# The last layer norm's shift row put into the outputs beforehand, and the outputs stored by accumulating transfers

## The reference

```
x = layer_norm(ALPHA * x + gate1 * mix, ln1_g, ln1_b)
ffn = expert_choice_ffn(x * (1 + scale2) + shift2)
y = layer_norm(ALPHA * x + gate2 * ffn, ln2_g, ln2_b)

layer_norm(x, g, b) = (x - mean(x)) * rsqrt(var(x) + 1e-6) * g + b      # mean and var over the 2048 columns
```

## Time and profile before

| | |
|---|---|
| runs of the kernel | 2162.7, 2165.96 and 2167.95 us, median 2165.96 us |
| the profiled execution | 2165.0 us, of which the span from the first to the last instruction is 2163.4 us |
| busy in the span | PE 2042.6 us (94%), DVE 1000.5 us (46%), ACT 202.6 us (9%), POOL 115.4 us (5%) |
| moved by DMA | 649.10 MB, mean 300 GB/s |
| experts (1163 to 2104 us) | DMA engines' busy share 0.99, 421 GB/s |
| from 2137.0 to 2160.2 us | DVE busy 21.81 of 23.20 us, PE 3.46, ACT 3.46, POOL 10.51 |

### The profile page before, as it was taken

How to read it: one execution, slowest core, us unless ns; L and a number is a source line. 1 busy time by engine, 2 the same in 40 slices (tenths; PEclk the granted TensorE clock), 3 DMA queues, 4 the chain that set the end, 5 groups by cost and what they waited for, 6 DMA issues and landing times.

```text
span 2163.4 us, 21990 instructions
## 1 busy us (share of the span) xinstructions
PE 2042.6 (94%) x9427; PEld 1198.9 (55%) x9427; DVE 1000.5 (46%) x1359; ACT 202.6 (9%) x482; POOL 115.4 (5%) x166
## 2 busy tenths in 40 slices
PE   6999999999999999999999999999999999998995
PEld 3455455555799999999784433333333333332221
DVE  3321256638699899898653351121112222222126
ACT  2111310000011111111011200000000000000000
POOL 1010010002010000100100100000000000000001
PEclk8999999999999999999999999999999999999998
DMA  9993027513277666666758799999999999999994
GB/s 342 403 363 117 0 72 263 196 57 107 78 234 241 227 232 230 217 230 229 283 198 348 307 396 433 431 431 431 431 430 431 431 432 430 430 425 436 427 422 178
DMA packets 141851, 649.10 MB, mean 300 GB/s; under 512 B 7314, under 2 KB 83996, under 8 KB 118650
## 3 DMA queue, kind: packets, MB, share of 16 engines
q1 hardware_dynamic: 129698, 586.05, 68.1%
q0 software_dynamic: 11568, 61.57, 8.0%
q10 hardware_dynamic: 488, 0.08, 0.0%
HBM read 641.15 MB, written 6.52 MB: 299 GB/s over the span
## 4 chain that ended last, share of the span: by engine, by line
PE 71%; DMA 19%; DVE 7%; SPq 1%; ACT 1%; issue 1%; DVEq 0%; ACTq 0%
DMA ring<-in_w_up_dram 13%; PE ps L976 12%; PE ps L1310 11%; PE ps L1355 8%; PE ps L1519 8%; PE ps L982 6%; PE ps L1042 4%; DMA ring<-in_w_down_dram 4%; PE ps L1097 3%; PE ps L913 2%; PE ps L785 2%; PE ps L750 1%; PE ps L797 1%; PE ps L1229 1%; DMA ring<-in_w_ada_dram 1%; PE ps L1495 1%
## 5 line engine op out<-in xcount | busy, mean ns | idle before, releaser
L1310 PE MATMUL ps<-ring,arena 128*64 128x512 f32 x2016 | 458.3, 599 | 32.3 <-DMA ring<-in_w_gate_dram 21.7
L1310 PEld LDWEIGHTS ps<-ring,arena 128*64 128x64 f32 x2016 | 140.7, 137 | 337.5 <-issue 273.8
L2564 DVE TENSOR_TENSOR arena<-ps,arena 128x512 f32<-128x512 f32 x180 | 116.0, 686 | 380.2 <-PE ps L1229 380.2
L1355 PE MATMUL ps<-ring,arena 128*64 128x512 f32 x960 | 212.9, 601 | 7.8 <-DMA ring<-in_w_down_dram 6.5
L1901 DVE SCALAR_TENSOR_TENSOR arena<-ring,arena 128x2048 f32<-128x2048 f32 x90 | 211.4, 2349 | 2.1
L976 PE MATMUL ps<-arena,ring 128*128 128x192 f32 x1024 | 174.4, 326 | 0.1
L976 PEld LDWEIGHTS ps<-arena,ring 128*128 128x128 f32 x1024 | 167.6, 190 | 1.5 <-issue 1.2
L1519 PE MATMUL ps<-arena,ring 128*128 128x384 f32 x512 | 165.6, 486 | 0.0
L1355 PEld LDWEIGHTS ps<-ring,arena 128*64 128x64 f32 x960 | 67.9, 138 | 141.1 <-issue 129.1
L1519 PEld LDWEIGHTS ps<-arena,ring 128*128 128x128 f32 x512 | 97.2, 190 | 68.2 <-issue 0.9
L976 PE MATMUL ps<-ring 128*128 128x192 f32 x768 | 132.7, 326 | 0.0
(11 more groups left out here) (381 smaller groups left out, 1831.9 us busy)
## 6 DMA issues: line engine op xcount, KB each, us to landing
ring<-in_w_gate_dram SPq DMA_DIRECT2D x28, 4096.0 KB, 20.4
ring<-in_w_up_dram SPq DMA_DIRECT2D x28, 4096.0 KB, 20.4
ring<-in_w_down_dram SPq DMA_DIRECT2D x28, 4096.0 KB, 20.7
ring<-in_w_in_dram SPq DMA_DIRECT2D x29, 2048.0 KB, 8.7
ring<-in_w_ada_dram POOLq DMA_DIRECT2D x48, 1024.0 KB, 5.2
ring<-in_w_ada_dram SPq DMA_DIRECT2D x32, 1024.0 KB, 17.9
ring<-in_w_out_dram SPq DMA_DIRECT2D x16, 2048.0 KB, 8.9
ring<-in_w_ada_dram SPq DMA_DIRECT2D x8, 2048.0 KB, 13.0
```

The costliest lines, as they stand in the source:

```text
L1310: mm = pe.matmul(ps[j // 4][64 * half:64 * half + m, :], xe_w[g % 2][:, c0:c0 + m], w[:, k4, half * 512:(half + 1) * 512], start=(k == 0), ...
L1355: mm = pe.matmul(ps[3 + u % 2][64 * half:64 * half + 64, :], hidT[:, k % 4, 64 * (k // 4):64 * (k // 4) + 64], w[:, k2, u * 512:(u + 1) * ...
L2564: dve.tensor_tensor(out, ps[SCATTER_BANKS[q % 5]][:, :], out, ALU.add).then_inc(S["cb_used"], 1)
```

## The change

The shift row b no longer goes through an engine at the end. During the gate stage SP writes `ln2_b` into all 384 rows of the two outputs, in three transfers from DRAM to DRAM of 1 MB each, one ahead of each of the loads `ga` 4, 5 and 6. At the end the half tiles, now without b, are stored by transfers that add to what the output holds. They are issued by POOL. DVE does (x - mean) * g for all three tiles, one pass a block, and ACT multiplies each half tile by r (with a bias column of zeros). POOL's four products and sums, DVE's four shifts and the load and the copying of `ln2_b` are gone. ACT takes all three square roots before the first of its six products.

```diff
+                    if kind == "ga" and 4 <= b < 7:
+                        sp.dma_start(out_rows(b - 4), t["ln2_b"][0].partition_broadcast(P)).then_inc(st_ahead, 16)
...
-            for ready, count, tile, half in (("out_mid", 1, 0, 0), ("out_ready", 1, 1, 0), ("out_ready", 2, 1, 1),
-                                             ("out_mid", 2, 0, 1), ("out_ready", 3, 2, 0), ("out_ready", 4, 2, 1)):
-                dst = y_prompt[0] if tile == 0 else y_sample[0, (tile - 1) * P:tile * P, :]
-                cs = slice(half * 1024, (half + 1) * 1024)
-                sp.wait_ge(S[ready], count)
-                sp.dma_start(dst[:, cs], acc[:, tile, cs]).then_inc(st_out, 16)
...
-            pool.dma_start(ln2[0:1, 1, :], row(t["ln2_b"][0], 1)).then_inc(ld_ln2, 16)
-            pool.wait_ge(ld_ln2, 32)
-            for kind in range(2):
-                pool.partition_broadcast(ln2[:, kind, :], ln2[0:1, kind, :]).then_inc(gp, 1)
-            pool.wait_ge(gp, 8)
-            for half in range(2):
-                cs = slice(half * 1024, (half + 1) * 1024)
-                pool.wait_ge(S["scaled_g"], 2 * half + 2)
-                pool.tensor_tensor(acc[:, 0, cs], acc[:, 0, cs], ln2[:, 0, cs], ALU.mult).then_inc(gp, 1)
-                pool.wait_ge(gp, 9 + half)
-                pool.tensor_tensor(acc[:, 0, cs], acc[:, 0, cs], ln2[:, 1, cs], ALU.add).then_inc(S["out_mid"], 1)
+            pool.wait_ge(ld_ln2, 16)
+            pool.partition_broadcast(ln2[:, 0, :], ln2[0:1, 0, :]).then_inc(gp, 1)
+            pool.wait_ge(st_ahead, 112)
+            for tile in range(3):
+                for half in range(2):
+                    cs = slice(half * 1024, (half + 1) * 1024)
+                    pool.wait_ge(S["out_ready"], 2 * tile + half + 1)
+                    pool.dma_start(out_rows(tile)[:, cs], acc[:, tile, cs], accum_op=ALU.add).then_inc(st_out, 16)
...
             for tile in range(3):
                 act.wait_ge(S["var_done"], 4 + tile)
                 act.activation(lnv[:, tile, 2:3], lnv[:, tile, 2:3], ACT.Sqrt).then_inc(S["std_done"], 1)
-                if tile < 2:
-                    act.wait_ge(S["scaled"], 1)
-                    for u in (2 * tile, 2 * tile + 1):
-                        rows = acc[:, 0, u * 512:(u + 1) * 512]
-                        act.activation(rows, ps[LAST_BANKS[0, u]][:, :] if u % 2 else rows, ACT.Identity,
-                                       bias=lnv[:, 0, 4:5], scale=lnv[:, 0, 3:4]).then_inc(S["scaled_g"], 1)
+            for tile in range(3):
+                act.wait_ge(S["scaled"], tile + 1)
+                for half in range(2):
+                    cs = slice(half * 1024, (half + 1) * 1024)
+                    act.wait_ge(S["drained"], 4 * tile + 2 * half + 2)
+                    act.activation(acc[:, tile, cs], acc[:, tile, cs], ACT.Identity,
+                                   bias=iota[:, 0:1], scale=lnv[:, tile, 3:4])\
+                       .then_inc(S["out_ready"], 1)
...
             def last_norms():
                 last_stats(0)
+                dve.wait_ge(gp, 7)
+                last_gain(0, 0)
+                last_gain(0, 1)
                 last_scale(0)
-                link(dve.scalar_tensor_tensor(lnv[:, 0, 4:5], lnv[:, 0, 0:1], -1.0, lnv[:, 0, 3:4], ALU.mult, ALU.mult))
-                dve.sem_inc(S["scaled"], 1)
                 last_stats(1)
-                dve.wait_ge(gp, 8)
-                last_gain(1, 0)
-                last_gain(1, 1)
+                last_gain(0, 2)
+                last_gain(0, 3)
+                last_scale(1)
                 last_stats(2)
-                last_scale(1)
-                last_shift(1, 0)
-                last_gain(1, 2)
-                last_gain(1, 3)
+                for u in range(4):
+                    last_gain(1, u)
                 last_scale(2)
-                last_gain(2, 0)
-                last_shift(1, 1)
-                last_gain(2, 1)
-                last_gain(2, 2)
-                last_shift(2, 0)
-                last_gain(2, 3)
-                last_shift(2, 1)
+                for u in range(4):
+                    last_gain(2, u)
```

More of the change, by code:

```diff
@@ L409, in contexts_of, with out_rows @@
             return ps[CTX_BANKS[k // 4]][:, k % 4 * 64:(k % 4 + 1) * 64].rearrange("p (a b) -> p a b", b=CAP_C)
+        def out_rows(tile):
+            return y_sample[0, (tile - 1) * P:tile * P, :] if tile else y_prompt[0]
         def xe_count(e):
@@ L583, in _ @@
             load_bada(2)
[L585 removed]
+            pool.wait_ge(st_ahead, 64)
             pool.dma_start(ckv[:, 1, :], t["cache_kv_c"][0, 0]).then_inc(ld_att, 16)
@@ L2593, in last_scale @@
                 dve.wait_ge(S["std_done"], 4 + tile)
-                link(dve.reciprocal(lnv[:, tile, 3:4], lnv[:, tile, 2:3]))
+                dve.reciprocal(lnv[:, tile, 3:4], lnv[:, tile, 2:3]).then_inc(S["scaled"], 1)
             def last_gain(tile, u):
@@ L2601, in last_gain @@
                                          ALU.subtract, ALU.mult).then_inc(S["drained"], 1)
-            def last_shift(tile, half):
-                cs = slice(half * 1024, (half + 1) * 1024)
-                dve.wait_ge(S["drained"], 4 * (tile - 1) + 2 * half + 2)
-                dve.scalar_tensor_tensor(acc[:, tile, cs], acc[:, tile, cs], lnv[:, tile, 3:4], ln2[:, 1, cs],
-                                         ALU.mult, ALU.add).then_inc(S["out_ready"], 1)
             def last_norms():
                 last_stats(0)
+                dve.wait_ge(gp, 7)
+                last_gain(0, 0)
+                last_gain(0, 1)
                 last_scale(0)
-                link(dve.scalar_tensor_tensor(lnv[:, 0, 4:5], lnv[:, 0, 0:1], -1.0, lnv[:, 0, 3:4], ALU.mult, ALU.mult))
-                dve.sem_inc(S["scaled"], 1)
                 last_stats(1)
-                dve.wait_ge(gp, 8)
-                last_gain(1, 0)
-                last_gain(1, 1)
+                last_gain(0, 2)
+                last_gain(0, 3)
+                last_scale(1)
                 last_stats(2)
-                last_scale(1)
-                last_shift(1, 0)
-                last_gain(1, 2)
-                last_gain(1, 3)
+                for u in range(4):
+                    last_gain(1, u)
                 last_scale(2)
-                last_gain(2, 0)
-                last_shift(1, 1)
-                last_gain(2, 1)
-                last_gain(2, 2)
-                last_shift(2, 0)
-                last_gain(2, 3)
-                last_shift(2, 1)
+                for u in range(4):
+                    last_gain(2, u)
             dve.wait_ge(ld_mods, 128)
```

11 lines of the change are left out of this document (5 added, 6 removed).

## The result

The changed kernel takes 2177.0 us (median of five runs, 2172.87 to 2184.51) against 2165.96 before: a ratio of 1.0062, 95% interval 1.0047 to 1.0077. It is slower by 0.5 to 0.6% (1.0062 goes by all runs; the two medians alone have a quotient of 1.0051). The forecast was no change, with 2167.3 us and a range up to 2176.0.

A forecast was written before the change was run, and what follows sets the result against it. DVE's list of work plus one store was taken to bound the kernel. The 7.1 us gained by ACT and DVE were lost in the DMA engines' store queue, +1.9 us on 2165.4: 2167.3 us, range 2160.0 to 2176.

The forecast's parts named there:

- The bound, and the waiting for POOL: At the end, DVE's last 22.6 us plus one store set the time; 5.9 us of them are waiting for POOL.
- DVE's and ACT's lists: At the end, DVE's last gain is done at 2151.1, 9.0 us sooner; ACT's last product at 2153.0, 7.1 sooner.
- The lower bound for a product: ACT's products of 1024 columns at the end: at least 1.07 us from one to the next; 1.15 was taken.
- The fills: Gate stage: each fill takes 2.4 us of the DMA engines, at zero cost; the rival that they delay PE had 0.04.
- my outer bound of 4.9: Gate stage: a fill takes 4.9 us of the DMA engines if its read and write don't overlap.
- The cover of 9 us: Gate stage: a load may be about 9 us late before PE stands.
- The rate of an accumulating store: Stores at the end: 2.43 us of all DMA engines for each accumulating store, as for 1 MB read.
- The queue of stores: At the end, stores issued each 1.15 us queue up at 2.43 us each; the last lands at 2164.65.
- With 0.6 us after that the span ends at 2165.3.: End of the span: 0.6 us follow the last store's landing, so it ends at 2165.3, +1.9 us.
- slow stores: Rival, stores at the end: reads and write don't overlap, 3.65 us of the engines each, 2174.6 us in all; chance 0.26.

The follow-up runs named there:

- e2: Changed kernel with plain instead of accumulating stores, issued by SP instead of POOL; output lacks b: 2162.9 us against 2163.9 before.
- e5: Kernel before with only the changed last norms, stored plainly by SP, no fills; output lacks b: 2161.35 us against 2162.76, ratio 0.9990.
- e3: Kernel before with the three fills of the outputs alone: 2163.89 us against 2163.9, ratio 1.0001.
- e1: Changed kernel with plain instead of accumulating stores, still issued by POOL; output lacks b: 2172.54 us against 2163.9 before.
- e7: Changed kernel with three accumulating stores of 1 MB instead of six of half a tile: 2174.2 us against 2162.76 before.
- e6: Kernel before with one more POOL store of 4 KB when the last half tile is ready: 2176.68 us against 2162.76.
- e12: e4 with one POOL product of 16 columns last on its queue: 2165.97 us against 2164.72 before.
- e14: Changed kernel with one POOL product of 16 columns behind its last accumulating store: 2174.15 us against 2164.72 before.
- e11: Kernel before with tiles 0 and 1 stored by POOL's accumulating stores, tile 2 by DVE's shifts and SP: 2170.2 us against 2164.24.
- e13: e5 with one POOL product of 16 columns last on its queue; output lacks b: 2159.46 us against 2164.72 before, ratio 0.9966.
- e10: The same kernel as e4, unaltered, with more runs: 2165.5 us against 2164.24 before.
- e15: e4 with two POOL products of 16 columns, one right after the row copies and one last: 2160.62 us against 2164.17 before, ratio 0.9983.
- e4: Kernel before with only tile 0 done the new way (one fill, two accumulating POOL stores): 2162.1 us against 2163.9.
- e9: e5 with four tiny SP stores, one after the other, behind the last; output lacks b: 2165.1 us against 2164.24 before.

## Why the prediction was wrong, point by point

**The bound, and the waiting for POOL: right.** The gains and shifts were long because of POOL's products. With those gone every gain takes 0.74 us.

**DVE's and ACT's lists: right.** The last gain was to end 13.6 us into the tail and did so at 13.3; ACT's six products were to end at 15.5 and did at 14.9, one each 1.13 us. (The lower bound for a product, 0.597 + 0.43, is 1.03 and not 1.07; nothing hung on it.) The first store was to go out at 9.9 and went at 9.9. Stored plainly by SP this end saves 6.4 to 6.9 us of tail (e2, e5); I had said 7.1 for the last half tile's readiness.

**The fills: right in the result, mis-sized.** A fill costs 5.5 us to land and delays the load by 6.4 us, not the 2.4 that I took from a load of one row into SBUF; that is above my outer bound of 4.9, too. The cover of 9 us held (e3: no change).

**The rate of an accumulating store: right.** I took 2.43 us of the engines from POOL's plain loads of 1 MB. From the second on the stores landed 2.6 us apart on average, at about 200 GB/s, where plain stores of the same bytes moved 382 and 383 GB/s (e1, e2). That is a factor of 1.9. The Trainium skill ("Collectives: The Full Stack", the part on the bandwidth ceiling) has 1.93 for a reducing transfer against a plain one and puts it down to two read descriptors on one ring: the trace agrees with the factor, and doesn't show the descriptors.

**The queue of stores: mis-sized by 3.5 us.** The term "the first lands at 2147.4 + 5.1, and five more behind it at 2.43 each" puts the last landing 17.25 us behind the first issue; it was 20.7. The first landed after 5.5 us, at 2162.0, the second 5.0 us behind it, and the other four 2.4 to 2.8 apart. In 1 MB pieces it was 17.6 (e7). Why the second came so late stays open.

**The step that failed: "With 0.6 us after that the span ends at 2165.3."** I carried the 0.6 us between landing and end over from SP's stores to POOL's. It was 5.4 us, 4.8 more. I priced an accumulating transfer with care and took the change of the issuing queue to be worth 1.3 us of fixed time. The runs show in its place POOL's DRAIN: the program ends no sooner than 10.3 us after POOL's last instruction, be it a store, a transfer of 4 KB or a product (e1, e6, e12, e14), and no sooner than 5.3 us after the landing of an accumulating store of POOL's (changed, e7, e11). Together with the 3.5 us this gives the missing 8.2 us of tail (36.0 against the forecast 27.8). The rival "slow stores" had the sign, but not the mechanism: no store took 3.65 us of the engines.

**What no term stood for: PE's clock, and POOL's state at the start.** In kernels whose POOL doesn't end with plain compute, the time ahead of the tail is longer by 1 to 8 us, at a lower mean clock. For the changed kernel itself it shows as 0.9 us between the difference of the medians and that of the tails, against five runs of before, and as 1.6 us between it and e14; it isn't resolved there. In e5 against e13 and in e10 against e15 it is 4 to 5 us; the intervals of the second pair don't overlap, those of the first do, by 0.0003.

That it acts through the start of the next execution is shown by a sharper sign than the first transfer. POOL's first product of an execution, here in e5 and in e13:

```profile
521.85 3.42 POOL L637 TENSOR_TENSOR ring<-arena 128x1536 f32<-128x1536 f32 x1 [9.07 <-issue]
```

```profile
511.45 3.46 POOL L637 TENSOR_TENSOR ring<-arena 128x1536 f32<-128x1536 f32 x1 [0.36 <-issue]
```

Up to there the two programs are the same; they differ only after the copying of the rows at 1900. In all nine kernels whose POOL computes nothing after that copying (changed, e1, e2, e4, e5, e7, e9, e10, e11) this product comes after 8.4 to 9.2 us of idle time that begins with the two records seen in e12; in the other eight kernels the same two records stand there and 0.35 or 0.36 us pass. So what was last computed on POOL is carried into the next execution, and the change from copying to products is paid there when it wasn't paid before. PE's work that lies between 500 and 600 us takes 1.9 to 3.1 us longer in the nine than in the kernel before, and 0 to 1.7 in the others: in the nine the granted clock falls to 1.2 GHz for 3.4 to 6.8 us at about 545 us. That is some 2 us of the 4 to 5. The rest isn't located (between 1000 and 1300 us profiles of both kinds lose 0 to 5 us), nor is the way from the late product to PE's clock; e6, whose product isn't late, still lies 5.9 us above its tail in four runs.

## What to carry to other kernels

When a transfer moves to another queue, price the end of that queue, too: here a last transfer from GpSimd cost 5 to 8 us of silence that one from SP did not, so GpSimd should be finished some 10 us before the span's end, and its accumulating stores, at half the rate of plain ones, should come first and not last. When an end gets shorter and the median doesn't follow, compare the mean clock at equal tails before looking for a stall, and look at how GpSimd's last computation leaves it for the next execution. And take out of the way of VectorE what GpSimd computes beside it; that was the real gain here, and e15 keeps it.

## What the hardware did that was not expected

- The span ends no sooner than 10.3 us after POOL's last instruction, and no sooner than 5.3 us after the landing of its last accumulating store. The time is a DRAIN on POOL's queue (20.6 us long in the changed kernel).
- POOL stands idle for 8.4 to 10.3 us between the copying of rows across partitions and its next plain product (e12 to e15), even when that product belongs to the next execution (nine kernels).
- An accumulating store takes 0.87 us to issue against 0.53 for a plain one on POOL, and moves 196 to 210 GB/s against 382.
- A product put last on POOL raised the mean clock of PE by 0.0019 to 0.0026 at equal tails, 4 to 6 us of 2160 (e13 against e5, e15 against e10, and with few runs e14 against the changed kernel).
